# Expert pairs of a mixture-of-experts stage: the eight overflow pairs at the end of the sequence instead of between the others

## The reference, cut to what matters

```
def expert_block(args):
    xb, e = args
    return (jax.nn.silu(xb @ w_gate_e[e]) * (xb @ w_up_e[e])) @ w_down_e[e]
...
y_slot = yb[dest] * w_f[order][:, None].astype(yb.dtype)
y = jnp.zeros((N, D), h.dtype).at[tok[order]].add(y_slot)
```

## Time and profile before

| | us |
|---|---|
| median of 3 runs (lowest, highest) | 3643.93 (3642.27, 3645.55) |
| the profiled execution's own time | 3636.73 |
| its span | 3634.9 |
| expert stage, first `gate_up` to start of the last position's `gate_up` | 3267.74 to 3569.77 |

### The profile page before, as it was taken

One profiled execution on the slowest core, in us unless ns is written; L12 is line 12 of the kernel. 1 busy time (PEld: TensorE's weight loads), 2 busy tenths in 40 slices (PEclk: granted clock), 3 DMA queues, 4 the chain that ended last, 5 costly groups with the idle time before them and its releaser, 6 DMA issues. The chain is left out here.

```text
span 3634.9 us, 36277 instructions
## 1 busy us (share of the span) xinstructions
PE 3210.1 (88%) x13724; PEld 2292.6 (63%) x13724; DVE 1448.0 (40%) x2284; ACT 882.5 (24%) x1408; POOL 147.2 (4%) x150
## 2 busy tenths in 40 slices
PE   2999999799887899998999898999897788969995
PEld 1888888446744377887888446888686465343332
DVE  6546455355176265554333203333321563131113
ACT  2211111311244132224322203322332254011111
POOL 0000000010010000000000000000000100002220
PEclk9999999899999999999999999999998789969997
DMA  4423322110100155542222102222223000327883
GB/s 168 155 90 115 129 85 104 59 46 35 46 0 0 46 218 208 193 164 91 90 101 85 67 23 93 90 98 87 84 98 116 3 0 12 139 104 297 327 354 137
DMA packets 78689, 395.84 MB, mean 109 GB/s; under 512 B 17280, under 2 KB 18688, under 8 KB 52608
## 3 DMA queue, kind: packets, MB, share of 16 engines
q1 hardware_dynamic: 67072, 386.10, 28.4%
q0 software_dynamic: 11520, 8.43, 0.8%
HBM read 444.80 MB, written 16.78 MB: 127 GB/s over the span
## 5 line engine op out<-in xcount | busy, mean ns | idle before, releaser
L554 PE MATMUL ps<-h_high_ffn,weights_high_ffn 128*128 128x512 f32 (+1 forms) x1696 | 624.9, 368 | 14.6 <-DVE weights_low_ffn L674 10.7
L555 PE MATMUL ps<-h_low_ffn,weights_high_ffn 128*128 128x512 f32 (+1 forms) x1696 | 624.2, 368 | 0.0
L556 PE MATMUL ps<-h_high_ffn,weights_low_ffn 128*128 128x512 f32 (+1 forms) x1696 | 623.6, 368 | 0.0
L631 ACT ACTIVATE weights_high_ffn<-weights 128x2048 fp32r<-128x2048 f32 (+4 forms) x168 | 259.5, 1545 | 471.7 <-PE ps L556 396.9
L674 DVE TENSOR_TENSOR weights_low_ffn<-weights,weights_high_ffn 128x2048 fp32r<-128x2048 f32 (+4 forms) x168 | 308.0, 1834 | 145.3 <-ACT weights_high_ffn L631 143.1
L554 PEld LDWEIGHTS ps<-h_high_ffn,weights_high_ffn 128*128 128x128 f32 x1696 | 320.5, 189 | 69.4 <-DVE weights_low_ffn L674 10.6
L555 PEld LDWEIGHTS ps<-h_low_ffn,weights_high_ffn 128*128 128x128 f32 x1696 | 320.7, 189 | 53.0
L556 PEld LDWEIGHTS ps<-h_high_ffn,weights_low_ffn 128*128 128x128 f32 x1696 | 320.5, 189 | 53.1
L554 PE MATMUL ps<-hidden_high_ffn,weights_high_ffn 128*128 128x512 f32 (+1 forms) x880 | 326.8, 371 | 17.4 <-DVE weights_low_ffn L674 10.1
L555 PE MATMUL ps<-hidden_low_ffn,weights_high_ffn 128*128 128x512 f32 (+1 forms) x880 | 325.8, 370 | 0.0
L556 PE MATMUL ps<-hidden_high_ffn,weights_low_ffn 128*128 128x512 f32 (+1 forms) x880 | 325.7, 370 | 0.0
(11 more groups left out here) (313 smaller groups left out, 4037.6 us busy)
## 6 DMA issues: line engine op xcount, KB each, us to landing
weights<-in_ffn_gu SPq DMA_DIRECT2D x88, 1024.0 KB, 4.9
big<-in_w_exp_gu SPq DMA_DIRECT2D x32, 2048.0 KB, 9.9
scratch_ffn<-in_w_mod SPq DMA_DIRECT2D x35, 1536.0 KB, 6.4
weights<-in_ffn_d SPq DMA_DIRECT2D x24, 768.0 KB, 4.2
weights<-in_w_in SPq DMA_DIRECT2D x16, 1024.0 KB, 4.8
weights<-in_ffn_d SPq DMA_DIRECT2D x24, 640.0 KB, 3.9
weights<-in_w_exp_dn SPq DMA_DIRECT2D x15, 1024.0 KB
hbuf<-in_w_exp_dn SPq DMA_DIRECT2D x12, 1024.0 KB
```

Of the source, the lines that this page charges most:

```text
L554: pe.matmul(out, wh, xh, start=(k == 0), stop=False)
L555: pe.matmul(out, wh, xl, start=False, stop=False)
L556: mm = pe.matmul(out, wl, xh, start=False, stop=(k == n - 1))
L631: scalar.activation(w_high[:, s, 0:n], ring.buf[:, s, 0:n], ACT.Copy).then_inc(high_done[s].sem, 1)
```

## The change

`SEQ` becomes 0, 1, 2, ..., 23: all sixteen ordinary pairs, then all eight overflow pairs. The overflow weights are counted on four semaphores of each kind instead of two, chosen by the block's number among the overflow blocks instead of by j.

```
-SEQ = []
-for n in range(EXPERTS // 2):
-    SEQ.append(n)
-    if n % 2 and n < EXPERTS // 2:
-        SEQ.append(EXPERTS // 2 + n // 2)
+SEQ = list(range(PAIRS))
 ORDER = [2 * n + b for n in SEQ for b in range(2)]
...
-    extra_gu_landed = [count(f"extra_gate_up_weights_landed{b}") for b in range(2)]
-    extra_dn_landed = [count(f"extra_down_weights_landed{b}") for b in range(2)]
+    extra_gu_landed = [count(f"extra_gate_up_weights_landed{b}") for b in range(4)]
+    extra_dn_landed = [count(f"extra_down_weights_landed{b}") for b in range(4)]
...
-                            .then_inc(extra_gu_landed[j % 2].sem, 16)
+                            .then_inc(extra_gu_landed[c % 4].sem, 16)
...
-                            .then_inc(extra_dn_landed[j % 2].sem, 16)
+                            .then_inc(extra_dn_landed[c % 4].sem, 16)
...
-                        pe.wait_ge(extra_landed[j % 2].sem, 16 * ((ORDER[j] - EXPERTS) // 2 + 1))
+                        pe.wait_ge(extra_landed[ORDER[j] % 4].sem, 16 * ((ORDER[j] - EXPERTS) // 4 + 1))
```

## The result

| | before | after |
|---|---|---|
| median of 4 runs (lowest, highest), us | 3643.41 (3642.27, 3645.55) | 3675.23 (3670.52, 3682.31) |
| profiled execution, its time / span, us | 3636.73 / 3634.9 | 3675.79 / 3673.9 |

The kernel became slower by 31.8 us: ratio 1.0089, 95% interval 1.0077 to 1.0101. The forecast was 3675 us, 3662 to 3692.

A forecast was written before the change was run, and what follows sets the result against it. TensorE sets the pace before, at 12.81 us a position; real pairs back to back are bound by the weight stream at 16.2 us. +30.0 us for the stage and +1 for the clock on 3643.93 give 3675 us, range 3662 to 3692.

The forecast's parts named there:

- The step that decides: Expert stage: real pairs back to back need 16.2 us of DMA against 12.81 of TensorE, which waits up to position 15.
- The rival of a sagging stream: Weight stream cannot hold its burst rate for 220 us; at 344 GB/s +79 us, 3723 us; 5 in 100.
- The sum in the profiled execution: Expert stage: position 15's weights land, then eight empty pairs take 102.5 us; position 23 starts at 3599.8, +30.0 us.
- the two ends: Weight stream up to position 15: 3.5 us for start, landing and wake-up, 1.5 us for a restart after position 2.
- The clock: TensorE's clock falls after waits in real pairs; free at positions 5 to 14, 1 us added in all.
- The 1 us put on position 15: Slow start of gate_up at position 15 is on the path: 1.7 us at better than even odds, entered as 1 us.
- POOL: Empty pairs' loads stand together at the end, under 8 us of POOL work per 12.81 us position; cost 0.
- the model: Expert stage: real pairs back to back arrive at the stream's pace; an empty pair is free only while the stream has something to bring.

The follow-up runs named there:

- run 8: Changed kernel with 3 spare matmuls ahead of the wait of gate_up at positions 5 to 15; 3677.26 us beside 3645.76, ratio 1.0090.
- run 5: Changed kernel with the eight overflow pairs left out (16 positions); 3572.35 us beside 3646.18, ratio 0.9805.
- run 1: Changed kernel with the overflow pairs in front, order 0, 1, the eight overflow pairs, then 2 to 15; 3683.55 us beside 3646.18, ratio 1.0104.
- run 9: Changed kernel with both gate-and-up loads of a pair issued ahead of both down loads; 3673.68 us beside 3643.06, ratio 1.0086.
- run 10: Kernel before the change with both gate-and-up loads of a pair issued ahead of both down loads; 3637.74 us beside 3643.06, ratio 0.9987.
- run 7: Changed kernel with 11 spare matmuls ahead of the wait of gate_up at positions 5 to 15; 3749.97 us, ratio 1.0296.

## Why the prediction was right, point by point

- *The step that decides.* TensorE catches up with the stream at position 5 and waits up to position 15: so it was (3343.74, 17.3 us after position 4). The pace was forecast at 16.2 us and measured at 16.4. The rate was 420 GB/s for 200 us, forecast 421. The rival of a sagging stream is refuted; so is, here, the figure of about 358 GB/s for one core that the Trainium skill gives in "DMA: Bandwidth & Descriptors", section "Where 436 GB/s comes from".
- *The sum in the profiled execution.* Position 0 to 23 was forecast to take 332.1 us (3599.8 - 3267.74), with 1 us more for the clock, and took 337.35. Of the 5.3 us over 332.1, 1.4 are the first `gate_up`, 9.79 against 8.40 us: the granted clock over it was 0.72 instead of 0.84. It took 8.42 to 10.04 us in the runs above, so this is scatter, and the forecast had no term for it. The other 3.9 lie between the first loads and position 15, 225.0 us instead of 221.2: 2.4 of them up to position 5, 1.4 in the ten positions after it. Part is at the start: position 2 asks for less, and the first two windows of the changed kernel show 405 and 327 GB/s. Part is at the end, where the last 9 us ahead of position 15 run at 272 GB/s. I had given the two ends 5.0 us. What thins the end was not tried; it stays open.
- *The clock.* It falls in the long waits, and the cost is hidden, as forecast. The 1 us put on position 15 was not paid: it waited 2.37 us and its `gate_up` took 7.09. The forecast also had every wait at 2 to 4 us; in fact they alternate, 4.25, 0.15, 3.85, 1.26, and only after the long ones is `gate_up` slow (9.92, 8.78). So the rule of the Trainium skill ("TensorE: Matmul & The Clock Gate", section "HAM oscillation — how this bites in real kernels"), by which every pair would start slow, holds here for about every second pair. Starts of real pairs are uneven without clock falls as well (15.7 to 17.3 us apart in run 8, 15.4 to 17.6 in the changed kernel), so the clock does not make that; its cause was not looked for.
- *POOL.* Its groups of loads at eight positions in a row cost nothing: 12.82 us each, no wait. The rows around position 17 show the room left, its loads issued by 3519.94 and its use at 3532.80:

```profile
3515.04 1.02 POOL L2271 DMA_INDIRECT big<-in_w_exp_gu,extra_rows  x1 [7.65 <-PE ps L2322]
3516.36 0.99 POOL L2277 DMA_INDIRECT hbuf<-in_w_exp_dn,extra_rows  x1 [0.31 <-issue]
3517.65 0.99 POOL L2271 DMA_INDIRECT big<-in_w_exp_gu,extra_rows  x1 [0.31 <-issue]
3518.95 0.99 POOL L2277 DMA_INDIRECT rope<-in_w_exp_dn,extra_rows  x1 [0.30 <-issue]
```

- *How exact.* The median moved by 31.8 us for 31 forecast, while the one profiled execution moved by 39.1 and the stage in it by 35.3. The difference is not in the expert stage alone: position 0 starts 4.6 us later after, and among the runs above, whose programs up to there are nearly the same, it starts anywhere from 3267.37 (run 5) to 3278.72 (run 1). A hit within 1 us is partly luck: for the stage itself the forecast was 4 us short. What is solid is the mechanism, and the stage's length to within those 4 us. For three further orders the model gave it within 2 us (341.69, 314.09, 321.54), but by then it had the changed kernel's trace to go by, and its pace was set to 16.3 us.

## What to carry to other kernels

Where a stage has work that needs transfers and work that needs none, count both per item (here 16.2 us of stream and 12.81 of TensorE for a real pair, 0 and 12.81 for an empty one) and mix them so that neither resource runs dry for longer than the buffers (here two positions of gate-and-up weights) can bridge. Sorting them apart makes the two bounds add. Of the orders tried, two real to one empty was the quickest: it cost 302 us here, one to one with six real pairs left over 314, half of the empty ones at the end 322, all apart 337 and 342. Whether another mix is quicker still was not tried. Where the stream was full, the order of loads within it hardly counted (run 9); where it idled between bursts, putting first what is waited for first gained 5 us (run 10).

## What the runs showed of the hardware that was not expected

- The trace shows each fp32 matmul as two rows. At the full clock 11 matmuls of 128x512 with a 128*128 stationary operand took 9.71 us, 0.88 us each, and 16 with a 128*64 one 7.07 us, 0.44 us each. This does not say that a narrow matmul alone is quicker: in run 7 the median row lasted 0.59 us with either operand. The narrow ones here fill the two halves of the output by turns, and in `down` of run 7, where the two weights lie in different buffers and the rows stay apart, the two halves start 0.03 us after each other and the next two 0.43 us later:

```profile
3361.06 0.59 PE L2348 MATMUL ps<-weights,work 128*64 128x512 f32 x1
3361.09 0.59 PE L2348 MATMUL ps<-hbuf,work 128*64 128x512 f32 x1
3361.49 0.59 PE L2348 MATMUL ps<-weights,work 128*64 128x512 f32 x1
```

- How long TensorE waited does not alone decide whether the clock falls: a wait of 2.37 us was followed by a `gate_up` of 7.09 us in the changed kernel (position 15) and by one of 8.78 us in run 5 (position 4). Slow starts at a wait added 1.4 us (8.51 against 7.09, position 13 of the changed kernel) to 3.0 us (10.05, run 1).
- The stream carried 420 GB/s for 200 us with no sag; its last 9 us ran at 272, with the DMA engines 0.68 busy.
